# Attention with unscaled probabilities, streams that meet only their own keys, and output halves stored apart

## The chip, the cores and the metric

The kernel runs on one core of a Trainium2 chip. The metric is the device time of one execution in microseconds (us), taken as the median over several runs. Lower is better. A profile is one execution recorded by the hardware profiler.

## What is computed

One inference step of a two-layer encoder, for a prompt of 1024 frames and for 8 running streams of 16 new frames each (128 rows together). Layer one uses forgetting attention (causal, with a cumulative log-forget bias), layer two uses banded attention in chunks of 64 frames with a learned bias by distance. Each is followed by an output projection and a gated feed-forward block.

```python
def fox_attention_prompt(q, k, v, logf):            # 16 heads of 64, blocks of 128 queries
    s = einsum('bqhd,bkhd->bhqk', qb, k) * scale
    s = s + cq[..., :, None] - cum[..., None, :]
    s = where(key_pos[None, :] <= qpos[:, None], s, NEG_INF)
    p = softmax(s, axis=-1)
    return einsum('bhqk,bkhd->bqhd', p, v)
# streams: the same, each stream's 16 queries against its own 128 cached keys and its 16 new ones
h = h + merge_heads(attention(q, k, v, ...)) @ w_out
h = h + swiglu(rms_norm(h, g_ffn), w_gate_up, w_down)
```

## The kernel before

The program is a row of blocks, with a barrier of all engines between them: projections of the first layer, the first attention ("fox" in the names), its output projection ("aout"), feed-forward, projections of the second layer, the second attention ("band"), its output projection ("bout"), feed-forward. Every product is done to more than single-pass accuracy: an operand is split in a high and a low part, and the parts are multiplied apart.

**attention_block** (lines 783 to 1287) works head by head. A head has nine units: S, which holds the 128 stream rows, and eight prompt tiles of 128 queries, here t0 to t7. A prompt tile meets 1 to 8 key tiles in fox, 1 to 5 in band. S meets nine key tiles at once (the 8 streams' caches and the tile of new keys), and everything that is not a stream's own is masked by a third matmul of each piece (L1236, `own` against `others`). 18 units of two heads form a pair, and a hardware loop (`Fori`) goes over the pairs. Each engine runs its own program of steps, and unit n passes through it in stages that lag behind each other:

- TensorE (PE): `score(n)` at step n, into `sp_wide` or `sp_slim` in turns; four steps later `turn` transposes the probabilities, up to four tiles in one bank of `tp` (three banks); `values` six steps later multiplies them with the values, for two prompt tiles (a group) or for S. In a step the order is turn, score, values. The output bank `op` is the tail of `sp_wide`, so S's scores wait for it too.
- VectorE (DVE): `tensor_tensor_reduce` adds the bias and takes the row maximum (L1203); later a reciprocal (L1182) and, in fox, the scaling of the probabilities by it (L1185); `low` (L1174) makes the low part of the transposed probabilities; L1212 adds the two halves of the output.
- ScalarE (ACT): `high` (L1115), the exponential with its row sum (L1150), the copy of half the output (L1156), the high part of the values (L1126).
- GpSimd (POOL): in fox the bias of each unit (L1048, L1058, L1060) and the masked diagonals (L1033), in band the scaling (L1077); the low part of the values (L1024).
- SyncE (SP) issues the loads of each head (`load_head`), of the values of a pair (`load_values`) and the stores of the output (`store_head`), in the order of its program; each waits on semaphores.

**Turned** (lines 195 to 232) is the source of the output projection: it loads one token tile of the turned attention output (L219, 512 KB), and splits it (L224 on ACT, L228 on DVE). `dense_block` multiplies tile by tile, two chunks of 512 output columns, 24 matmuls for a tile and chunk.

## Time and profile before

| | us |
|---|---|
| median of 3 runs | 3515.49 |
| lowest and highest run | 3514.15, 3516.90 |
| span of the profiled execution | 3516.8 |
| first attention, 404 to 856 | 452 |
| first output projection, 866 to 968 | 102 |
| second attention, 2176 to 2540 | 364 |

The page gives PE as 91% busy, DVE 42%, ACT 33%, POOL 12% over the whole span. These averages mix dense blocks, in which PE never waits, with the two attentions, in which several engines share the work. So the stages are read apart: by windows of time, by the groups of instructions inside one window, and by the timeline of single instructions. In the timeline a record's end includes the way through the engine, and the next record of the same engine may begin some hundredths of a microsecond earlier.

### The profile page before, as it was taken

How to read it: one execution, taken by the hardware profiler on the slowest of the kernel's cores; microseconds unless marked ns; L12 is line 12 of the kernel's file. 1: busy time of each engine (PE TensorE's matmuls, PEld its weight loads, DVE VectorE, ACT ScalarE, POOL GpSimd, SP SyncE). 2: the span in 40 equal slices, each digit the busy share in tenths (PEclk: the TensorE clock that was granted, in tenths of full speed). 3: DMA queues.
4: the chain of work that ended last, by engine and by line, in shares of the span. 5: the costliest groups of instructions: out<-in, count | busy, mean ns of one | idle time of the engine just before them, and what ended most of it. 6: DMA issues, size and time to landing. Idle time of an engine off the chain costs nothing. (4 is left out here: it accounts for less than half of the span.)

```text
span 3516.8 us, 47851 instructions
## 1 busy us (share of the span) xinstructions
PE 3217.5 (91%) x16000; PEld 2680.0 (76%) x16000; DVE 1489.9 (42%) x2930; ACT 1174.2 (33%) x2540; POOL 423.7 (12%) x686
## 2 busy tenths in 40 slices
PE   8999577776999999999989997888699999999998
PEld 7877366665878888888878886777677888888887
DVE  3121388887243333333332221776634333333333
ACT  4232266665142211112223323777623122111122
POOL 0000245542000000000000001444300000000000
PEclk9999799998999999999999998999999999999999
DMA  4885343452441111111014884444322111111111
GB/s 153 200 250 166 137 153 141 153 178 74 125 156 60 48 36 36 36 36 52 19 51 144 241 213 160 158 157 160 106 84 78 37 51 56 36 36 36 36 36 54
DMA packets 329715, 363.82 MB, mean 103 GB/s; under 512 B 25200, under 2 KB 270976, under 8 KB 323344
## 3 DMA queue, kind: packets, MB, share of 16 engines
q1 hardware_dynamic: 329616, 362.52, 32.8%
q8 instruction: 60, 0.98, 0.1%
q14 instruction: 39, 0.32, 0.0%
HBM read 255.23 MB, written 120.98 MB: 107 GB/s over the span
## 5 line engine op out<-in xcount | busy, mean ns | idle before, releaser
L251 PE MATMUL ffn_gu<-ffn_gh,ffn_xh 128*128 128x512 f32 x1584 | 635.2, 401 | 0.0
L253 PE MATMUL ffn_gu<-ffn_gh,ffn_xl 128*128 128x512 f32 x1584 | 619.6, 391 | 0.0
L252 PE MATMUL ffn_gu<-ffn_gl,ffn_xh 128*128 128x512 f32 x1584 | 619.3, 391 | 0.0
L1517 DVE TENSOR_TENSOR all_h<-ffn_dn,all_h 128x1024 f32<-128x1024 f32 x198 | 242.4, 1224 | 354.3 <-PE ffn_dn L253 354.3
L1501 DVE TENSOR_TENSOR ffn_hid<-ffn_gu,ffn_gate 128x256 f32<-128x256 f32 x198 | 83.8, 423 | 722.2 <-ACT ffn_gate L1494 722.2
L1494 ACT ACTIVATE ffn_gate<-ffn_gu 128x256 f32<-128x256 f32 x198 | 75.7, 382 | 833.0 <-PE ffn_gu L253 833.0
L253 PEld LDWEIGHTS ffn_gu<-ffn_gh,ffn_xl 128*128 128x128 f32 x1584 | 298.0, 188 | 63.1
L252 PEld LDWEIGHTS ffn_gu<-ffn_gl,ffn_xh 128*128 128x128 f32 x1584 | 298.9, 189 | 56.8
L251 PEld LDWEIGHTS ffn_gu<-ffn_gh,ffn_xh 128*128 128x128 f32 x1584 | 298.4, 188 | 56.0
L251 PE MATMUL ffn_dn<-ffn_dh,ffn_hidh 128*128 128x512 f32 x792 | 308.4, 389 | 2.9 <-DVE ffn_hidl L1512 2.9
L253 PE MATMUL ffn_dn<-ffn_dh,ffn_hidl 128*128 128x512 f32 x792 | 309.0, 390 | 0.0
L252 PE MATMUL ffn_dn<-ffn_dl,ffn_hidh 128*128 128x512 f32 x792 | 308.2, 389 | 0.0
L1508 ACT ACTIVATE ffn_hidh<-ffn_tps 128x256 fp32r<-128x256 f32 x198 | 75.6, 382 | 438.1 <-PE ffn_tps L1472 438.1
L251 PEld LDWEIGHTS ffn_dn<-ffn_dh,ffn_hidh 128*128 128x128 f32 x792 | 148.7, 188 | 34.1 <-DVE ffn_hidl L1512 3.3
L251 PE MATMUL qkvw_acc<-qkvw_h,qkv_xh 128*128 128x512 f32 x432 | 173.5, 402 | 0.0
L251 PE MATMUL band_inw_acc<-band_inw_h,band_in_xh 128*128 128x512 f32 x432 | 172.7, 400 | 0.0
L253 PEld LDWEIGHTS ffn_dn<-ffn_dh,ffn_hidl 128*128 128x128 f32 x792 | 148.6, 188 | 30.9
L252 PEld LDWEIGHTS ffn_dn<-ffn_dl,ffn_hidh 128*128 128x128 f32 x792 | 148.7, 188 | 30.8
L1269 PE MATMUL fox_tp<-all_ident,fox_pr 128*128 128x128 f32 x720 | 125.4, 299 | 49.5 <-DVE fox_ptl L1174 29.3
L253 PE MATMUL qkvw_acc<-qkvw_h,qkv_xl 128*128 128x512 f32 x432 | 169.9, 393 | 0.0
L252 PE MATMUL qkvw_acc<-qkvw_l,qkv_xh 128*128 128x512 f32 x432 | 169.3, 392 | 0.0
L253 PE MATMUL band_inw_acc<-band_inw_h,band_in_xl 128*128 128x512 f32 x432 | 169.2, 392 | 0.0
(231 smaller groups left out, 6066.2 us busy)
## 6 DMA issues: line engine op xcount, KB each, us to landing
ffn_graw<-in_w_gate_up SPq DMA_DIRECT2D x40, 1024.0 KB, 7.5
ffn_draw<-in_w_down SPq DMA_DIRECT2D x22, 1024.0 KB, 4.9
fox_ks<-k_split SPq DMA_DIRECT2D x16, 1088.0 KB, 5.6
fox_ncb<-negcum SPq DMA_DIRECT2D x16, 1088.0 KB, 10.1
band_ks<-k_split SPq DMA_DIRECT2D x16, 1088.0 KB, 5.5
qkvw_raw<-in_w_a_in SPq DMA_DIRECT2D x5, 2048.0 KB, 9.6
out<-qkvw_stage SPq DMA_DIRECT2D x36, 256.0 KB, 3.2
q_high<-qkvw_th SPq DMA_DIRECT2D x72, 128.0 KB, 2.5
```

The costliest lines, as they stand in the source:

```text
L251: pe.matmul(out, xh, wh, start=first, stop=False)
L252: pe.matmul(out, xh, wl, start=False, stop=False)
L253: return pe.matmul(out, xl, wh, start=False, stop=last)
L1269: last = pe.transpose(tp[:, (base + k) % TB, b * P:(b + 1) * P], pr[slot_of[n]][:, (j + b) * P:(j + b + 1) * P], ident[:])
L1494: act.activation(gate[:], gu[:, t % 2, 0:GW], ACT.Silu).then_inc(gate_ready, 1)
L1501: dve.tensor_tensor(hid[:], gu[:, t % 2, GW:2 * GW], gate[:], ALU.mult).then_inc(hid_ready, 1)
L1508: act.activation(hidh[:].rearrange("p c n -> p (c n)"), tps[:, 0:GW], ACT.Copy).then_inc(hidh_ready, 1)
L1517: dve.tensor_tensor(h[:, t, :], dn[:].rearrange("p a n -> p (a n)"), h[:, t, :], ALU.add).then_inc(dn_used, 1)
```

## The change

In both attentions:

- The probabilities are not scaled. The row sums go into a new buffer `sums`, kept over the blocks, and `Turned` takes their reciprocals, spreads them over 64 columns of each head (POOL), turns them (PE, 8 transposes a tile) and multiplies them into the loaded output (DVE).
- S meets 2 key tiles in place of 9. `begin` computes each stream's scores against its own cache (8 matmuls of 32 moving columns, L1208), ACT and DVE add the two parts, and `score` turns the result back; the new keys are one more tile. `values` for S has 2 matmuls of 128 columns and 16 of 16 columns.
- The output leaves `op`, now a bank of its own, by one DVE copy (L1184) with both halves, which are stored apart. `Turned` loads two halves of 512 KB and POOL adds them.
- The values' high part moves from ACT to POOL; `split_values(hd+1)` stands in fox's POOL program between the bias of t5 and that of t6 of head hd, and waits for the load of the values when hd+1 is even.
- The loop over pairs is gone: all 16 heads are written out, S first in every head. Lags are shorter: turn 3 steps, values 5, output 6. In a PE step the order is turn, begin, values, score. The exponential of a unit stands in the same ACT step as its maximum in DVE's.
- fox loads the stream part of the bias by nine small transfers; SP's order is `load_values`, `load_head(hd + 2)`, `store_head(hd)`.

The core of the diff:

```diff
     def rsqrt(self, pool, t):
-        pass
+        s = t % 3
+        if t == 0:
+            pool.wait_ge(self.inv_ready, 1)
+        if t >= 2:
+            pool.wait_ge(self.spread, 2 * (t - 1))
+        pool.tensor_copy(self.rows[:, t % 2], self.inv[:, t, :].rearrange("p (u o) -> p u o", o=1)
+                         .to_broadcast([P, HEADS, HD])).then_inc(self.rows_ready, 1)
+        pool.wait_ge(self.loaded[s], 32 * (t // 3 + 1))
+        pool.tensor_tensor(out=self.raw[:, s, 0], in0=self.raw[:, s, 0], in1=self.raw[:, s, 1],
+                           op=ALU.add).then_inc(self.added, 1)
 
     def scaled(self, dve, t):
-        pass
+        if t == 0:
+            dve.reciprocal(self.inv[:], self.sums[:]).then_inc(self.inv_ready, 1)
+        dve.wait_ge(self.added, t + 1)
+        for half in range(2):
+            part = self.raw[:, t % 3, 0, 4 * half:4 * half + 4, :]
+            dve.wait_ge(self.spread, 2 * t + half + 1)
+            dve.tensor_tensor(part, self.ptr[:, half, :].rearrange("p (c n) -> p c n", c=4), part,
+                              ALU.mult).then_inc(self.scaled_done, 1)
...
     def fetch(self, sp, t):
-        if t >= 2:
-            sp.wait_ge(self.low_ready, t - 1)
-        sp.dma_start(self.raw[:, t % 2], self.src[:, t * P:(t + 1) * P].rearrange("(c p) n -> p c n", p=P)
-                     ).then_inc(self.loaded[t % 2], 16)
+        if t >= 3:
+            sp.wait_ge(self.low_ready, t - 2)
+        for u in range(2):
+            sp.dma_start(self.raw[:, t % 3, u], self.src[u, :, t * P:(t + 1) * P].rearrange("(c p) n -> p c n", p=P)
+                         ).then_inc(self.loaded[t % 3], 16)
...
+    UH = NT
+    N = HEADS * UH
+    GH = 1 + QT // 2
+    LT, LV, LO = 3, 5, 6
...
+                    sp.dma_start(f32(ks[b][:]), ks_d[hd]).then_inc(kq_loaded[b], 16)
+                    sp.dma_start(f32(q2[b][:, 0, :]), qh_d[hd]).then_inc(kq_loaded[b], 16)
+                    sp.dma_start(f32(q2[b][:, 1, :]), ql_d[hd]).then_inc(kq_loaded[b], 16)
...
 
                 def load_values(p):
-                    wait(sp, vl_done, 2 * NV * p)
+                    if p:
+                        sp.wait_ge(vl_done, 2 * p)
                     for at, n, src in v_parts:
-                        sp.dma_start(vraw[:, at:at + n, :], src(bass.ds(p * P, P))).then_inc(v_loaded, 16)
+                        sp.dma_start(vraw[:, at:at + n, :], src(slice(p * P, (p + 1) * P))).then_inc(v_loaded, 16)
+
+                def store_head(hd):
+                    sp.wait_ge(o_done, GH * (hd + 1))
+                    for u in range(2):
+                        sp.dma_start(out_d[u, hd * HD:(hd + 1) * HD, :], att[hd % 2][u * HD:(u + 1) * HD, :]
+                                     ).then_inc(att_stored[hd % 2], 16)
...
+                load_head(1)
+                for hd in range(HEADS):
+                    if hd % 2 and hd + 1 < HEADS:
+                        load_values((hd + 1) // 2)
+                    if hd + 2 < HEADS:
+                        load_head(hd + 2)
+                    store_head(hd)
...
+                def split_values(hd):
+                    b, at = hd % 2, hd % 2 * HD
+                    if b == 0:
+                        pool.wait_ge(v_loaded, 16 * len(v_parts) * (hd // 2 + 1))
+                    if hd >= 2:
+                        pool.wait_ge(pv_done, GH * (hd - 1))
+                    pool.tensor_copy(vs[b][:, :, 0:HD], vraw[:, :, at:at + HD]).then_inc(vh_done, 1)
+                    pool.wait_ge(vh_done, hd + 1)
+                    pool.tensor_tensor(out=vs[b][:, :, HD:P], in0=vraw[:, :, at:at + HD],
+                                       in1=f32(vs[b][:, :, 0:HD]), op=ALU.subtract).then_inc(vl_done, 1)
...
+                    for n in range(N):
+                        hd, i = head_of(n), tile_of(n)
+                        if i == S:
+                            diagonal(hd)
+                            if hd == 0:
+                                split_values(0)
+                        else:
+                            unit_bias(n)
+                        if i == 5 and hd + 1 < HEADS:
+                            split_values(hd + 1)
+                        if i == 6 and hd + 1 < HEADS:
+                            fox_streams(hd + 1)
...
+                for s in STEPS:
+                    n = turned_at(s)
+                    if n is not None:
+                        high(n, True)
+                    if 0 <= s - 1 < N:
+                        exp(s - 1)
+                    if n is not None:
+                        high(n, False)
+                    if begun_at(s) is not None:
+                        begun(begun_at(s))
...
+                for s in STEPS:
+                    if 0 <= s - 1 < N:
+                        maximum(s - 1)
+                    n = turned_at(s)
+                    if n is not None:
+                        low(n, True)
+                    if group_at(s, LO) is not None:
+                        out(group_at(s, LO))
+                    if n is not None:
+                        low(n, False)
+                    if begun_at(s) is not None:
+                        begun(begun_at(s))
...
+                def begin(hd):
+                    b, r = hd % 2, begun_round[hd]
+                    pe.wait_ge(kq_loaded[b], 48 * (hd // 2 + 1))
+                    if r >= TB:
+                        pe.wait_ge(tl_done, r - TB + 1)
+                    for x in range(STREAMS):
+                        at = S * P + x * NEW
+                        last = pe.matmul(tp[:, r % TB, 2 * NEW * x:2 * NEW * (x + 1)],
+                                         ks[b][:, (QT + x) * P:(QT + x + 1) * P], q2[b][:, :, at:at + NEW],
+                                         start=True, stop=True)
+                    last.then_inc(t_done, 1)
...
+                def values(g):
+                    hd, tiles = g // GH, tiles_of(g)
+                    v = vs[hd % 2]
+                    pe.wait_ge(vl_done, hd + 1)
+                    if g:
+                        pe.wait_ge(o_done, g)
+                    pe.wait_ge(tl_done, rounds_through(last_unit(g)))
                     if g % GH == 0:
-                        pe.wait_ge(vl_done, (2 * p + hh + 1) * NV)
-                    wait(pe, o_done, p * G + g)
-                    if scored is not None:
-                        pe.wait_ge(max_done, scored)
-                    pe.wait_ge(tl_done, p * R + rounds_through(last_unit[g]))
+                        for y, buf in enumerate(group_slots(g)):
+                            pe.matmul(op[:, 0:P], v[:, KT - 1, :], buf[:, P:2 * P], start=y == 0, stop=False)
+                        for x in range(STREAMS):
+                            for y, buf in enumerate(group_slots(g)):
+                                last = pe.matmul(op[:, x * NEW:(x + 1) * NEW], v[:, QT + x, :],
+                                                 buf[:, x * NEW:(x + 1) * NEW], start=False,
+                                                 stop=x == STREAMS - 1 and y == 1)
...
+                for s in STEPS:
+                    if turned_at(s) is not None:
+                        turn(turned_at(s))
+                    if begun_at(s) is not None:
+                        begin(begun_at(s))
+                    if group_at(s, LV) is not None:
+                        values(group_at(s, LV))
+                    if 0 <= s < N:
+                        score(s)
```

On DVE, in fox, these rows stood where the first head of a pair works on t4 to t6 (`pr` the probabilities, `bias` the bias, `sp_wide` and `sp_slim` the scores, `mneg` the negated maximum):

```order
L1203 ISA fox_pr1,fox_mneg<-fox_sp_wide,fox_bias0 128x640
L1203 ISA fox_mneg 128x1
L1212 TENSOR_TENSOR fox_att<-fox_sp_wide,fox_half_out 64x256
L1174 TENSOR_TENSOR fox_ptl<-fox_tp,fox_pth 128x2x128
L1182 RECIPROCAL fox_inv<-fox_rowsum 128x1
L1185 TENSOR_SCALAR fox_pr0<-fox_pr0,fox_inv 128x512
L1203 ISA fox_pr2,fox_mneg<-fox_sp_slim,fox_bias1 128x768
L1203 ISA fox_mneg 128x1
L1174 TENSOR_TENSOR fox_ptl<-fox_tp,fox_pth 128x3x128
L1182 RECIPROCAL fox_inv<-fox_rowsum 128x1
L1185 TENSOR_SCALAR fox_pr1<-fox_pr1,fox_inv 128x640
L1203 ISA fox_pr3,fox_mneg<-fox_sp_wide,fox_bias0 128x896
```

And these stand there now, at t6 and t7 and the start of the next head:

```order
L1174 ISA fox_pr,fox_mneg<-fox_score,fox_bias 128x896
L1174 ISA fox_mneg 128x1
L1148 TENSOR_TENSOR fox_ptl<-fox_tp,fox_pth 128x4x128
L1184 COPY fox_att0<-fox_op 128x256
L1148 TENSOR_TENSOR fox_ptl<-fox_tp,fox_pth 128x128
L1154 TENSOR_TENSOR fox_whole_st<-fox_tp,fox_half_st 128x128
L1174 ISA fox_pr,fox_mneg<-fox_score,fox_bias 128x1024
L1174 ISA fox_mneg 128x1
L1148 TENSOR_TENSOR fox_ptl<-fox_tp,fox_pth 128x4x128
L1148 TENSOR_TENSOR fox_ptl<-fox_tp,fox_pth 128x2x128
L1174 ISA fox_pr,fox_mneg<-fox_score,fox_bsm1 128x256
```

The reciprocal and the scaling are gone. In one step now stand the maximum of a unit, the low parts of the unit two before it (its second part last) and, before the maximum of t7, the sum of the next head's stream scores (L1154).

On PE, in fox, before, where S of the second head is multiplied with the values (`sth` and `stl` S's probabilities, `pth` and `ptl` a group's, `vs` the values):

```order
L1233 MATMUL fox_sp_slim<-fox_ks1,fox_qh1 128x512
L1234 MATMUL fox_sp_slim<-fox_ks1,fox_ql1 128x512
L1233 MATMUL fox_sp_slim<-fox_ks1,fox_qh1 128x256
L1234 MATMUL fox_sp_slim<-fox_ks1,fox_ql1 128x256
L1269 MATMUL fox_tp<-all_ident,fox_pr4 128x128 x3
L1233 MATMUL fox_sp_wide<-fox_ks1,fox_qh1 128x512
L1234 MATMUL fox_sp_wide<-fox_ks1,fox_ql1 128x512
L1233 MATMUL fox_sp_wide<-fox_ks1,fox_qh1 128x384
L1234 MATMUL fox_sp_wide<-fox_ks1,fox_ql1 128x384
L1258 MATMUL fox_sp_wide<-fox_sth,fox_vs1 128x128
L1258 MATMUL fox_sp_wide<-fox_stl,fox_vs1 128x128
L1258 MATMUL fox_sp_wide<-fox_sth,fox_vs1 128x128
```

And now (`fox_score` the scores, `fox_op` the output bank), from the end of the values of t6 and t7:

```order
L1271 MATMUL fox_op<-fox_pth,fox_vs0 128x128
L1271 MATMUL fox_op<-fox_ptl,fox_vs0 128x128
L1230 MATMUL fox_score<-fox_ks1,fox_q21 128x512
L1231 MATMUL fox_score<-fox_ks1,fox_q21 128x512
L1241 MATMUL fox_tp<-all_ident,fox_pr 128x128 x2
L1254 MATMUL fox_op<-fox_sth,fox_vs1 128x128
L1254 MATMUL fox_op<-fox_stl,fox_vs1 128x128
L1257 MATMUL fox_op<-fox_sth,fox_vs1 128x16
L1257 MATMUL fox_op<-fox_stl,fox_vs1 128x16
L1257 MATMUL fox_op<-fox_sth,fox_vs1 128x16
```

The scores stood ahead of the values and stand behind them now; 16 of S's 18 value matmuls have 16 moving columns in place of 128, and their number is the same.

## Rows read from the trace of the kernel before

**Rows 1.** Windows: from:to, length; busy PE, PEld, DVE, ACT, POOL; PEclk, DMA share, GB/s.
```profile
404.00:856.00 452.00, 347.42 (x2176) 300.16 (x2176) 382.26 (x896) 277.35 (x656) 225.25 (x352) 0.90 0.41 146
866.00:968.00 102.00, 100.84 (x432) 82.93 (x432) 30.76 (x41) 16.58 (x23) 0.00 (x0) 0.97 0.43 126
2176.00:2540.00 364.00, 293.32 (x2016) 259.84 (x2016) 250.54 (x752) 268.93 (x689) 155.52 (x224) 0.95 0.44 148
```

**Rows 2.** Timeline, POOL, first attention: start us, us, work; every second mask of the diagonal.
```profile
506.89 1.09 POOL L1033 TENSOR_SCALAR_AFFINE_SELECT fox_diag<-fox_ncb 128x1024 f32<-128x1024 f32 x1 [0.23 <-POOL fox_bias L1060]
...
562.65 1.09 POOL L1033 TENSOR_SCALAR_AFFINE_SELECT fox_diag<-fox_ncb 128x1024 f32<-128x1024 f32 x1 [0.23 <-POOL fox_bias L1060]
```

**Rows 3.** Groups by form, DVE, 572 to 628 us: xcount | busy us, mean ns | idle.
```profile
L1174 DVE TENSOR_TENSOR fox_ptl<-fox_tp,fox_pth 128x512 fp32r<-128x512 f32 x13 | 8.9, 684 | 2.2 <-ACT fox_pth L1115 2.1
...
L1212 DVE TENSOR_TENSOR fox_att<-fox_sp_wide,fox_half_out 64x256 f32<-64x256 f32 x8 | 3.3, 416 | 0.5 <-ACT fox_half_out L1156 0.2
...
L1203 DVE CUSTOM_DVE_ANT_0 fox_pr<-fox_sp_slim,fox_bias 128x1024 f32<-128x1024 f32 x1 | 1.2, 1205 | 0.0
...
L1203 DVE CUSTOM_DVE_ANT_0 fox_pr<-fox_sp_slim,fox_bias 128x128 f32<-128x128 f32 x2 | 0.6, 278 | 0.0
```

**Rows 4.** The same view, ACT: exponential, reading of its sum, copy of turned scores.
```profile
L1115 ACT ACTIVATE fox_pth<-fox_tp 128x512 fp32r<-128x512 f32 x12 | 7.0, 595 | 7.9 <-PE fox_sp_wide L1258 4.4 <-PE fox_tp L1269 3.3
...
L1150 ACT ACTIVATION_READ_ACCUMULATOR fox_pr<-fox_pr,fox_mneg 128x1 f32 x18 | 3.4, 192 | 0.0
...
L1150 ACT ACTIVATE fox_pr<-fox_pr,fox_mneg 128x1024 f32<-128x1024 f32 x2 | 2.3, 1150 | 1.9 <-DVE fox_mneg L1203 1.9
...
L1150 ACT ACTIVATE fox_pr<-fox_pr,fox_mneg 128x128 f32<-128x128 f32 x2 | 0.8, 401 | 0.3 <-DVE fox_mneg L1203 0.3
```

**Rows 5.** Timeline, PE, first attention: consecutive matmuls, in three places.
```profile
607.03 0.41 PE L1258 MATMUL fox_sp_wide<-fox_pth,fox_vs 128*128 128x256 f32 x1
607.24 0.41 PE L1258 MATMUL fox_sp_wide<-fox_ptl,fox_vs 128*128 128x256 f32 x1
...
612.24 0.28 PE L1258 MATMUL fox_sp_wide<-fox_ptl,fox_vs 128*128 128x256 f32 x1
612.36 0.22 PE L1258 MATMUL fox_sp_wide<-fox_pth,fox_vs 128*128 128x128 f32 x1
612.42 0.28 PE L1258 MATMUL fox_sp_wide<-fox_ptl,fox_vs 128*128 128x128 f32 x1
...
616.14 0.28 PE L1258 MATMUL fox_sp_wide<-fox_sth,fox_vs 128*128 128x128 f32 x1
616.25 0.28 PE L1258 MATMUL fox_sp_wide<-fox_stl,fox_vs 128*128 128x128 f32 x1
```

**Rows 6.** DMA issues: xcount, KB each, median us from issue to landing.
```profile
fox_vraw<-in_cache_a_v SPq DMA_DIRECT2D x8, 512.0 KB, 5.6
...
aoutw_at<-attn_turned SPq DMA_DIRECT2D x9, 512.0 KB, 4.1
```

**Rows 7.** Groups by form, POOL, 572 to 628 us.
```profile
L1060 POOL TENSOR_SCALAR fox_bias<-fox_diag,fox_cqh 128x128 f32<-128x128 f32 x17 | 7.8, 458 | 1.5 <-DVE fox_mneg L1203 1.2 <-POOL fox_cqh L1036 0.3
...
L1024 POOL TENSOR_TENSOR fox_vs<-fox_vraw,fox_vs 128x384 fp32r<-128x384 f32 x4 | 4.0, 1003 | 0.4 <-ACT fox_vs L1126 0.4
...
L1058 POOL TENSOR_SCALAR fox_bias<-fox_ncb,fox_cqh 128x768 f32<-128x768 f32 x2 | 1.8, 908 | 2.2 <-DVE fox_mneg L1203 2.2
```

**Rows 8.** Timelines where the first projection begins: SP, PE and ACT.
```profile
856.87 0.40 SPq L219 DMA_DIRECT2D aoutw_at<-attn_turned  x1
...
866.39 0.80 PE L251 MATMUL aoutw_acc<-aoutw_h,aout_xh 128*128 128x512 f32 x1 [14.52 <-DVE aout_xl L228]
...
868.72 1.06 ACT L224 ACTIVATE aout_xh<-aoutw_at 128x1024 fp32r<-128x1024 f32 x1 [0.51 <-DMA aoutw_at<-attn_turned]
```

**Rows 9.** Groups by form, DVE, 572 to 628 us: the scaling of the probabilities.
```profile
L1185 DVE TENSOR_SCALAR fox_pr<-fox_pr,fox_inv 128x768 f32<-128x768 f32 x2 | 2.9, 1438 | 0.1
...
L1185 DVE TENSOR_SCALAR fox_pr<-fox_pr,fox_inv 128x1024 f32<-128x1024 f32 x3 | 2.3, 762 | 0.1
```

More of the change, by code:

```diff
@@ L312, in dense_block @@
             if turned_src is not None:
-                src = Turned(pw, turned_src, xh, xl)
+                src = Turned(pw, turned_src, xh, xl, ptr, ident, sums)
             else:
@@ L796, in width @@
     def width(i):
[L797 removed]
+        return 2 if i == S else (i + 1 if fox else min(i, BAND_TILES) + 1)
     def first_key(i):
[L800 to L808 removed]
@@ L856, in attention_block, with parts_of, turned_at @@
-    samples = [n for n, (_, i) in enumerate(order) if i == S]
-    values_step = [n + VALUES + ((n + VALUES) % U in samples) for n in last_unit]
-    out_step = [v + OUT - VALUES for v in values_step]
-    assert all(b > a for a, b in zip(values_step, values_step[1:])) and values_step[-1] < values_step[0] + U
+        return i + 1 - width(i)
+    def parts_of(i):
+        return [(j, min(4, width(i) - j)) for j in range(0, width(i), 4)]
+    def turned_at(s):
+        return s - LT if 0 <= s - LT < N else None
@@ new lines, in begun_at, with group_at @@
+    def begun_at(s):
+        return head_of(s + 1) if 0 <= s + 1 < N and tile_of(s + 1) == S else None
+    def group_at(s, lag):
+        n = s - lag
+        if not 0 <= n < N or n % UH % 2:
+            return None
+        return GH * head_of(n) + n % UH // 2
+    STEPS = range(-1, N + LO)
+    round_of, begun_round, r = {}, {}, 0
+    for s in STEPS:
+        n = turned_at(s)
+        if n is not None:
+            for j, _ in parts_of(tile_of(n)):
+                round_of[n, j] = r
+                r += 1
+        if begun_at(s) is not None:
+            begun_round[begun_at(s)] = r
+            r += 1
@@ L928, in pairs_loop @@
-        def pairs_loop(eng, steps):
-            steps(0, range(U), True)
-            with eng.Fori(1, PAIRS) as p:
-                steps(p, range(U), False)
-            steps(PAIRS - 1, range(U, out_step[-1] + 1), False)
-        def groups_at(p, first, step, steps_of):
-            for g, s in enumerate(steps_of):
-                if s == step:
-                    yield g, p
-                elif s == step + U and not first:
-                    yield g, p - 1
+        bias_done, diag_made, bsm_part, bsm_made = (ph.sem(x) for x in ("bias_done", "diag_made", "bsm_part", "bsm_made"))
@@ L1090, in band_pair @@
-                def band_pair(p, last=False):
-                    for n in range(U):
-                        if n == first_of_head[1] - 4:
-                            band_bias(p, 1)
-                        if n == U - 4 and not last:
-                            band_bias(p + 1, 0)
-                        normalise(p, n)
-                        values_low(p, n + NORM)
-                pair = fox_pair if fox else band_pair
-                if not fox:
-                    band_bias(0, 0)
@@ L1103, in _ @@
-                pair(0)
-                with pool.Fori(1, PAIRS - 1) as p:
-                    pair(p)
-                pair(PAIRS - 1, last=True)
+                pool.memset(own[:], 0.0).then_inc(own_made, 1)
+                pool.wait_ge(own_made, 1)
+                view = own[:].rearrange("p (b k) -> p b k", b=STREAMS)
+                pool.affine_select(out=view, in_=view, compare_op=ALU.is_ge, fill=NEG, base=0,
+                                   pattern=[[-NEW, STREAMS], [0, NEW]], channel_multiplier=1).then_inc(own_made, 1)
```

602 lines of the change are left out of this document (263 added, 339 removed).

## The prediction

> **What bounds the kernel now.** The windows of the three stages come first [rows 1]. In fox DVE is busy 382 of 452 us, PE 347, at a granted clock of 0.90: DVE is nearest to its limit. In band nobody is: PE 293, ACT 269, DVE 251 of 364. In the projection PE is busy 100.8 of 102. So a gain in an attention comes from shorter chains between engines, and any PE work or late start added to a projection costs its full time. The second view is the period of a pair: two masks of the diagonal with one between them are 55.8 us apart in fox [rows 2], 27.9 for a head; 16 heads are 446 us and about 6 are fill and drain. Band gives (364 - 6) / 16 = 22.4 us a head. The third is what single instructions take, which the chains below use [rows 3, 4, 5, 7].
>
> **What is removed.** The scaling took DVE 0.76 us for 1024 columns and 1.44 us for 768 [rows 9], so not its width but something beside it set its time. The Trainium skill ("SBUF — State Buffer", Who interferes with whom) says that a DVE instruction in a two-port mode and a GpSimd instruction lock each other out; the longer time of the narrower row agrees. By that rule the scaling's going speeds POOL as well, and it speaks against `Turned`: `low` reads two SBUF tensors there while POOL now adds, and by the rule each may wait up to a POOL instruction, 1 to 4 us a projection. The sum below leaves that out. DVE's own work is no longer a limit after the change, so I don't price the removal by work; I ask what chain is left.
>
> **The new chain, in steps.** I take one head of fox in steady state. A maximum of w tiles takes DVE 0.28 us at one tile and 1.21 at eight, so 0.13 more a tile; a low part 0.68 for four tiles and, as a maximum of the same width, 0.28 for one; the output copy 0.42 as the addition it replaces (nearest row, same columns) [rows 3]. An exponential takes ACT 0.40 to 1.15 and the reading of its sum 0.19; the copy of a high part 0.60 for four tiles and, taken as DVE's, 0.28 for one [rows 4]. I take off 0.05 for overlap of records and add 0.04 for a handover.
>
> In the four steps in which the transposed tile (t4 to t7) has a second part, DVE's next maximum waits for: maximum, exponential and reading, high of the second part, low of the second part. With the maximum of t6: 1.10 + 0.04 + 1.17 + 0.30 + 0.27 = 2.87, and 0.26 for the streams' sum: 3.13. With t7: 3.37. With S: 2.2. With t0: 2.14. Together 10.8 us. The other five steps go by DVE's work (maximum, low, output): 1.27, 0.80, 1.51, 1.79, 1.61, together 7.0. That would be 17.8 us a head.
>
> PE holds up two of these five, because the values now stand ahead of the scores and one bank holds the output. At full clock a matmul of 256 columns takes 0.12 us to the next start; one of 128 takes 0.06 behind one of 256, and 0.11 in the streams' row of matmuls of 128 [rows 5]. For those of 16 columns, which no row shows, the bounds are 0.06 and 0.11; I take 0.11, the row of the same place and order. Count from the start of the step with the maximum of t0. The output copy of t4/t5 ends at 3.4; the values of t6/t7 (14 of 0.12 and two more) end at 5.3; the scores of t3 (0.46) are complete at 5.95, where DVE could have begun at 4.2. DVE takes that maximum, a low part and the copy of t6/t7, until 7.45; then 18 stream matmuls, 2.0 us, the scores of t4, 0.68, and the way through the engine: 10.4, where DVE could have begun at 7.45. The two holds cost 1.75 and 2.95: **22.5 us a head**.
>
> The Trainium skill ("TensorE: Matmul & The Clock Gate", LDWEIGHTS) gives a weight load a time by its 128 columns, however few move after it, which fits the 0.11; its section Back-to-back issue gap gives a narrow matmul by itself some 25 ns, and by that the streams' values would take 0.5 us a head in place of 2.0 and the sum be 48 us less.
>
> **A wait that the change adds in fox.** POOL's `split_values` for an even head stands between the bias of t5 and of t6 of the head before, and waits for values that SP issues only after `store_head` of the head before that. In the count above: the copy of t6/t7 ends at 7.45; SP issues two stores and three loads, about 2 us; the last lands 5.6 us after its issue [rows 6]: 14.9. The high and low parts of 1088 columns, at 1.18 and 2.6 ns a column, take 4.1 us; the bias of t6 0.91 + 0.46 [rows 7]: 20.4. DVE needs it at 13.8. Queued behind the split on POOL are the biases of t6 and t7 and the next streams' bias; DVE, and through it everyone, waits **6.6 us**, seven times (for heads 2, 4 to 14). In between PE idles for some 7 us. In band no bias stands behind the split, and the values have a whole head's time: nothing.
>
> **Clock.** At the reduced clock of 1.2 GHz matmuls of 256 columns start 0.21 apart in place of 0.12 [rows 5], and fox had 0.90 on the mean [rows 1]. The 5.0 us of values and scores in the two holds would double. I allow 0.5 us a head in fox, 0.3 in band.
>
> Fox: 16 x 22.5 + 7 x 6.6 + 16 x 0.5 + 6 fill + 4 (the first values are split before the first prompt bias) = 424, against 452: **-28**.
>
> **Band.** Same steps with at most five tiles and a second part of one: 2.66, 2.40, 1.75, 1.41 and 1.25, 0.80, 1.51, 1.79, 1.47, together 15.0. Holds: t6/t7's values take 1.3, so the scores of t3 are there at 4.7 instead of 3.5; the streams' values and t4's scores at 9.1 instead of 6.2. 15.0 + 1.2 + 2.9 = 19.2; with the clock 19.5. 16 x 19.5 + 6 = 318, against 364: **-46**. POOL's scaling and ACT's spreading of the bias, half output and values go with it; they lay beside the chain.
>
> **Projections, twice.** Before, the first matmul came 9.5 us after the first load was issued, and the second tile landed 11.8 us after [rows 8], behind 3 MB (0.5 + 2 of weights + 0.5). Now 4 MB stand there: 15.2 us. DVE handles the second tile before it touches the weights, so the first matmul waits for it: addition on POOL 1024 x 2.6 ns = 2.7, two multiplications of 512 columns 1.3, two low parts of weights 1.3, `low` of 1024 columns 1.2 (all at the 0.68 of 512, less overlap), together 6.5: 21.7 us in place of 9.5, **+12.2**. Then 8 transposes a tile at 0.11 come ahead of PE's matmuls for seven of the nine tiles: **+6**. Per tile PE now takes 24 x 0.23 + 0.9 = 6.4 us (432 matmuls in 100.8 [rows 1]); POOL 3.8, DVE 3.3, and a buffer comes round in 10.5 us for two tiles, so none holds PE. Together +18.2, twice: **+36**.
>
> Everything else is untouched. The nine small bias loads add some 4 us of issue on SP a head, which has 22. The barrier and the stores (two in place of one) cost nothing that the fill doesn't hold. The load grows little: about 4.1 MB a head, at 22 us 186 GB/s against 146 now at a share of 0.41.
>
> Sum on the profiled span: 3516.8 - 28 - 46 + 36 = 3479. The span is 1.3 us above the median, so 3477 in the median's terms. I add 8 us, since every term of the chains is a lower count of waits: **3485 us**.
>
> **Rivals.**
> *The reduced clock stays.* The 6.6 us stalls and the short idle times leave PE at 1.2 GHz in the two holds of every fox head: 5.0 us more for each, less the 0.5 allowed: 16 x 4.5 = 72, 3557 us, slower than before. It decides from 31 / 16 = 1.9 us a head, that is with two fifths of the holds at the low clock. For it: a mean of 0.90 before, with shorter idle times. Against: PE is 70% occupied outside the stalls, where it was 60%.
> *The values arrive in time, or the stall hides.* If the load lands 6 us earlier or the split needs less, 7 x 6.6 = 46 fall away: 3439. For it: SP's own issue times are estimates. Against: the order of its program.
> *Narrow matmuls start closer.* At the lower bound, 0.06, the streams' values take 1.1 us in place of 2.0, and 32 x 0.9 = 29 fall away: 3456. For it: the 0.06 of rows 5. Against: that one's weights were loaded under a wider matmul, and none of the 16 has such cover.
> *The holds of PE don't bite*: 16 x (4.7 + 4.1) = 141 less, 3344, the lowest. Against it speak the order rows of PE: values ahead of scores, one bank.
> *The scaling does not leave the bound*, that is DVE's work before was hidden: excluded in fox by 382 of 452 us.
>
> **How the numbers follow.** Forecast 3485, between 3460 and 3520: 0.42. Narrow matmuls, 3450 to 3460: 0.08. Clock, 3520 to 3570: 0.22. No stall, 3405 to 3450: 0.20. No holds, below 3405: 0.05; beyond 3570: 0.03. The 80% range takes most of the clock case and of the one without stall: 3415 to 3555. A measurement can tell 0.2%, 7 us. The forecast case lies below 3508.5 with 0.34 of its 0.42; so faster: 0.34 + 0.08 + 0.20 + 0.05 = 0.67. Within 0.2%: its other 0.08 and the lowest 0.04 of the clock case, 0.12. Slower than 3522.5: 0.18 + 0.03 = 0.21.
>
> **What would show it.** In the changed profile: fox heads in pairs of about 22.5 and 29 us, DVE waiting for POOL's bias of t6 some 6 to 7 us, seven times; PE waiting for L1184 ahead of values; stream matmuls of 16 columns 0.11 apart; in the projections the first matmul some 22 us after the first load, 6.4 us a tile in the first chunk. Wrong it is if DVE never waits for a bias, if L1257 starts closer than 0.11, or if the granted clock of fox lies below 0.85.

## The result, and the profile after

| | before | changed |
|---|---|---|
| median of 4 runs, us | 3514.82 | 3579.72 |
| lowest and highest, us | 3513.67, 3516.90 | 3574.73, 3583.52 |
| span of the profiled execution, us | 3516.8 | 3578.5 |

The changed kernel is slower: ratio 1.0184, with a 95% interval of 1.0169 to 1.0198. I had forecast 3485, with a range of 3415 to 3555. The table compares the stages of the two profiled executions, each from the first load that it issues to that of the next stage. A stage of mine is that of before plus the terms of the prediction.

| stage, us | before | forecast | changed | off by |
|---|---|---|---|---|
| to the first attention | 396.3 | 396.3 | 398.1 | +1.8 |
| first attention | 460.6 | 432.6 | 445.5 | +12.9 |
| its output projection | 112.2 | 130.4 | 159.4 | +29.0 |
| feed-forward | 855.0 | 855.0 | 858.2 | +3.2 |
| projections of layer two | 343.8 | 343.8 | 343.2 | -0.6 |
| second attention | 375.4 | 329.4 | 349.4 | +20.0 |
| its output projection | 111.8 | 130.0 | 159.9 | +29.9 |
| feed-forward | 861.7 | 861.7 | 864.8 | +3.1 |
| span | 3516.8 | 3479 | 3578.5 | +99 |

Both attentions are faster than before, by 15 and 26 us, as forecast in sign and too small in size. The two projections lose 95 us, where I had 36. That is 59 us more than forecast, the larger part of the miss.

The windows answer to [rows 1], with the same columns: the first attention, the second, and the first half of the first projection and the rest of it.

```profile
405.00:842.00 437.00, 331.61 (x2096) 297.64 (x2096) 229.94 (x592) 209.56 (x513) 210.39 (x320) 0.84 0.45 146
...
2212.00:2552.00 340.00, 289.55 (x1936) 259.35 (x1936) 206.11 (x592) 187.37 (x513) 74.29 (x96) 0.90 0.53 175
...
868.00:936.00 68.00, 53.25 (x209) 42.43 (x210) 23.21 (x30) 6.34 (x6) 19.28 (x11) 0.84 0.44 124
936.00:1001.00 65.00, 62.85 (x281) 51.68 (x279) 16.36 (x23) 6.94 (x11) 0.00 (x0) 1.00 0.35 100
```

DVE has gone from 382 us to 230 in fox, so the scaling did leave. But the granted clock of PE is 0.84 where it was 0.90, and 0.90 where it was 0.95: more of PE's work runs at 1.2 GHz. In the projection's first 68 us PE is idle for 15; before it was idle for 0.4 of the first 51.

**The projection.** The timeline of PE, then of DVE, at tiles 1 and 2 of the first chunk (start, length, and in brackets the idle time and what ended it):

```profile
875.65 1.04 PE L243 MATMUL aoutw_ptr<-all_ident,aoutw_rows 128*128 128x128 f32 x8
878.92 0.51 PE L282 MATMUL aoutw_acc<-aoutw_h,aout_xh 128*128 128x512 f32 x1 [2.23 <-DVE aout_xl L259]
...
886.09 1.03 PE L243 MATMUL aoutw_ptr<-all_ident,aoutw_rows 128*128 128x128 f32 x8
889.36 0.68 PE L282 MATMUL aoutw_acc<-aoutw_h,aout_xh 128*128 128x512 f32 x1 [2.23 <-DVE aout_xl L259]
```

```profile
862.62 4.21 DVE L276 TENSOR_TENSOR aoutw_l<-aoutw_raw,aoutw_h 128x512 fp32r<-128x512 f32 x2
...
886.80 1.29 DVE L232 TENSOR_TENSOR aoutw_at<-aoutw_ptr,aoutw_at 128x512 f32<-128x512 f32 x2 [7.33 <-PE aoutw_ptr L243]
888.00 1.30 DVE L259 TENSOR_TENSOR aout_xl<-aoutw_at,aout_xh 128x1024 fp32r<-128x1024 f32 x1
```

PE turns the reciprocals of tile 3 (886.09) only after the matmuls of tile 1. DVE's program has the multiplication of tile 3 (L232, 886.80) ahead of the low part of tile 2 (L259, 888.00), so that low part, of a tile that had been multiplied 9 us before, waits for PE's transposes, and PE's next matmul waits for the low part. The round repeats about every 10.4 us (878.92 to 889.36), with 2.1 to 3 us of idle PE, and behind most of these holes 6 to 8 matmuls start 0.43 us apart in place of 0.23: the granted clock is at its lower level there. None of this stands in my working.

**The first attention.** DVE around the end of a stalled head and in the next one; `fox_bias` of 896 columns is t6's:

```profile
607.05 0.69 DVE L1174 CUSTOM_DVE_ANT_0 fox_pr<-fox_score,fox_bias 128x512 f32<-128x512 f32 x1 [2.07 <-PE fox_score L1231]
...
612.95 0.82 DVE L1174 CUSTOM_DVE_ANT_0 fox_pr<-fox_score,fox_bias 128x640 f32<-128x640 f32 x1 [4.51 <-PE fox_score L1231]
...
622.78 1.09 DVE L1174 CUSTOM_DVE_ANT_0 fox_pr<-fox_score,fox_bias 128x896 f32<-128x896 f32 x1 [5.72 <-POOL fox_bias L1043]
...
642.54 0.82 DVE L1174 CUSTOM_DVE_ANT_0 fox_pr<-fox_score,fox_bias 128x640 f32<-128x640 f32 x1 [3.97 <-PE fox_score L1231]
...
730.52 1.09 DVE L1174 CUSTOM_DVE_ANT_0 fox_pr<-fox_score,fox_bias 128x896 f32<-128x896 f32 x1 [9.05 <-issue]
...
744.47 0.69 DVE L1174 CUSTOM_DVE_ANT_0 fox_pr<-fox_score,fox_bias 128x512 f32<-128x512 f32 x1 [2.07 <-PE fox_score L1231]
...
748.89 0.82 DVE L1174 CUSTOM_DVE_ANT_0 fox_pr<-fox_score,fox_bias 128x640 f32<-128x640 f32 x1 [3.02 <-PE fox_score L1231]
...
765.90 0.69 DVE L1174 CUSTOM_DVE_ANT_0 fox_pr<-fox_score,fox_bias 128x512 f32<-128x512 f32 x1 [2.07 <-PE fox_score L1231]
```

And what t6's bias waited for, on SP and then on POOL:

```profile
608.47 1.09 SPq L987 DMA_DIRECT2D attn_turned<-fox_att  x2
609.61 0.77 SPq L982 DMA_DIRECT2D fox_vraw<-out  x1
610.42 1.52 SPq L982 DMA_DIRECT2D fox_vraw<-in_cache_a_v  x1
611.98 1.76 SPq L982 DMA_DIRECT2D fox_vraw<-out  x1
```

```profile
617.75 1.09 POOL L1010 CAST fox_vs<-fox_vraw 128x1088 fp32r<-128x1088 f32 x1 [11.73 <-DMA fox_vraw<-out]
618.93 2.49 POOL L1012 TENSOR_TENSOR fox_vs<-fox_vraw,fox_vs 128x1088 fp32r<-128x1088 f32 x1
621.40 0.91 POOL L1042 TENSOR_SCALAR fox_bias<-fox_ncb,all_cq 128x768 f32<-128x768 f32 x1
622.28 0.37 POOL L1043 TENSOR_SCALAR fox_bias<-fox_diag,all_cq 128x128 f32<-128x128 f32 x1
```

This is the chain of the prediction, step for step: stores, loads, split, bias. The wait came seven times, 5.28 to 9.05 us, 49.5 in all. The maximum of t3 waits 2.06 us for its scores and that of t4 3.02 to 4.9. Where the releaser reads "issue" (730.52), the profile names none; e2, further down, shows that this wait is of the same kind.

### The profile page after: what moved, and what is told of

It reads as the page before. It is cut to its first block and busy times, and to the rows that moved or that the text cites. A ratio compares the mean times of both kernels' runs of the same rounds, so it can differ in the third digit from the quotient of the medians.

```text
span 3578.5 us, 43068 instructions
## 1 busy us (share of the span) xinstructions
PE 3243.7 (91%) x15984; PEld 2709.1 (76%) x15984; DVE 1326.0 (37%) x2504; ACT 1021.2 (29%) x2216; POOL 386.5 (11%) x559
## 5 line engine op out<-in xcount | busy, mean ns | idle before, releaser
L283 PE MATMUL band_inw_acc<-band_inw_l,band_in_xh 128*128 128x512 f32 x432 | 168.7, 391 | 0.0
## 6 DMA issues: line engine op xcount, KB each, us to landing
qkvw_raw<-in_w_a_in SPq DMA_DIRECT2D x5, 2048.0 KB, 10.4
```

What stands on the lines that cost most here:

```text
L283: pe.matmul(out, xh, wl, start=False, stop=False)
```

## Experiments

Each kernel stands beside runs of the kernel before on the same chip, whose medians were 3517.85 (e1 to e4), 3516.85 (e5, c1, c2, e7) and 3516.70 (c3, c4, e8). "Against the changed kernel" means against its median of 3579.7, or stage by stage. A stage's time is that of one profiled execution, and it scatters: the first attention, whose code is the same in the changed kernel, e1 and e5, took 445.5, 448.8 and 440.0 us there, the second 349.4, 346.5 and 349.5. A second output bank for `op` was not tried.

**e1, the projection's order.**

```diff
-                                if t + 2 < NT:
-                                    src.scaled(dve, t + 2)
                                 if t + 1 < NT:
                                     src.low(dve, t + 1)
+                                if t + 2 < NT:
+                                    src.scaled(dve, t + 2)
```

> The changed kernel with one swap: in the first chunk of the two output projections DVE makes the low part of tile t+1 before it multiplies tile t+2 by the reciprocals. In the changed kernel a tile of that chunk takes 10.4 us: PE turns the reciprocals of tile t+1, then waits 2.23 us for DVE's low part of tile t, which stands behind the multiplication that waits for just these transposes, and then runs 8 or 9 matmuls at the reduced clock. Theory 1 (that loop is the cost): a tile takes 6.4 to 7 us, PE does not wait for L259 after the first tile, 8 x 3.7 = 30 us less in each projection, about 3520 us in all. Theory 2 (the load of two halves is the cost, POOL waits 7 us for each): a tile stays above 9 us, at most 10 us less in each, 3560 us or more. Theory 3 (the reduced clock would be there anyway): the holes go, the slow matmuls stay, 18 us less in each, about 3544 us.

Measured: 3521.6 us, ratio to before 1.0012 (1.0002 to 1.0022), 58 us less than the changed kernel. The projections take 133.1 and 132.9 in place of 159.4 and 159.9, which is 53 of the 58. PE, then DVE:

```profile
870.39 0.79 PE L282 MATMUL aoutw_acc<-aoutw_h,aout_xh 128*128 128x512 f32 x1 [12.76 <-DVE aout_xl L259]
...
878.13 1.03 PE L243 MATMUL aoutw_ptr<-all_ident,aoutw_rows 128*128 128x128 f32 x8
...
884.51 1.03 PE L243 MATMUL aoutw_ptr<-all_ident,aoutw_rows 128*128 128x128 f32 x8
```

```profile
878.84 1.29 DVE L232 TENSOR_TENSOR aoutw_at<-aoutw_ptr,aoutw_at 128x512 f32<-128x512 f32 x2 [3.76 <-PE aoutw_ptr L243]
...
881.25 3.46 DVE L259 TENSOR_TENSOR aout_xl<-aoutw_at,aout_xh 128x1024 fp32r<-128x1024 f32 x1 [0.53 <-ACT aout_xh L255]
```

PE turns every 6.4 us and waits no more. Theory 1 holds; theory 2 falls, since the load of two halves is still there and hidden; theory 3 falls, since the slow matmuls went with the holes.

**e5, the start as well.** e1, and `src.scaled(dve, 1)` behind `chunk_low` in the two output projections.

> The changed kernel with the swap of DVE's low part and multiplication in the first chunk (e1), and besides, in the output projections, DVE's multiplication of tile 1 moved behind the low parts of the first weights, so that nothing of tile 0 stands behind it. In the changed kernel and in e1 the first matmul starts 24.3 us after the first load. Theory 1 (it waits for the landing and the addition of tile 1, which DVE handles first): it starts 12 to 15 us after the first load, 9 to 12 us less in each projection, 20 in all against e1, about 3500 us. Theory 2 (the weights land that late anyway, behind the 1 MB of tile 0): the first matmul moves by under 3 us, 3515 to 3522.

Measured: 3500.5 us, 0.9954 (0.9937 to 0.9970), 21 less than e1. The first matmul starts 12.5 us after the stage's first load (833.7 and 846.2), and the stage takes 124.6 and 123.2, which is 8.5 and 9.7 less than in e1. Theory 1, at the low end of its 9 to 12.

**e2, the values early.**

```diff
-                    if hd % 2 and hd + 1 < HEADS:
-                        load_values((hd + 1) // 2)
+                    if hd % 2 == 0 and hd + 2 < HEADS:
+                        load_values(hd // 2 + 1)
```

> The changed kernel with one move on SP: the values of the next pair are loaded before the keys of head hd+2 and before the store of head hd (hd even), instead of after that store, one head later. Seven waits of DVE for the bias of t6, 5.3 to 9.1 us, stood in the changed kernel. Theory 1 (they come from the late load alone): all seven go, and with them part of the reduced clock, 50 to 65 us less in the first attention, 3515 to 3530 us in all; the pair of heads goes from 54 us to 45 to 47. Theory 2 (the queue only shifts: keys and biases of the next head, issued behind the values, are late instead): DVE or PE waits for keys or a bias of the next head, 10 to 30 us less, 3550 to 3570. Band: no change, within 3 us, by both.

Measured: 3532.8 us, 1.0042 (1.0025 to 1.0059), 47 less than the changed kernel; the first attention takes 400.3 in place of 445.5. The seven waits are gone and nothing came in their place. The second attention is 5.1 us shorter, more than the 3 that I allowed; part of that lies within the scatter given above. But the clock came back in small part only, 0.87 in the first attention where the changed kernel has 0.84:

```profile
403.00:790.00 387.00, 325.03 (x2096) 291.49 (x2096) 230.04 (x591) 209.20 (x513) 211.02 (x320) 0.87 0.50 162
```

```profile
447.77 0.82 DVE L1174 CUSTOM_DVE_ANT_0 fox_pr<-fox_score,fox_bias 128x640 f32<-128x640 f32 x1 [4.07 <-PE fox_score L1231]
...
588.54 0.82 DVE L1174 CUSTOM_DVE_ANT_0 fox_pr<-fox_score,fox_bias 128x640 f32<-128x640 f32 x1 [3.02 <-PE fox_score L1231]
```

In 10 of 15 heads the maximum of t4 still waits 4.1 to 4.8 us for its scores, in the others 3.02. So the stalls cost about what they last (45.2 us of 49.5), and most of the reduced clock is not their doing. Theory 1 for the wait, not for the clock.

**e3, scores ahead of values.** In PE's step `score(s)` stands before `values(...)`.

> The changed kernel with one swap on PE, in both attentions: in a step the scores stand ahead of the values. DVE waited for the scores of t3 2.06 us in every head of fox and 1.56 in band, for those of t4 3.0 to 4.9. Theory 1 (these are holds by the order on PE): both waits fall below 1 us; fox 16 x 4.5 = 72 us less, if no new wait comes, band 16 x 4 = 64 less; since PE's own work in band is some 260 us at full clock, and in fox the stalls for the bias stay, I expect 50 to 110 in all, 3470 to 3530 us. Theory 2 (PE's work is the bound, the order only moves the wait): the waits come back at other units, under 20 us less, 3560 to 3580.

Measured: 3523.5 us, 1.0018 (1.0008 to 1.0029), 56 less than the changed kernel: 24 in the first attention (421.7) and 30 in the second (318.9). DVE's waits:

```profile
439.43 0.42 DVE L1148 TENSOR_TENSOR fox_ptl<-fox_tp,fox_pth 128x256 fp32r<-128x256 f32 x1 [1.60 <-ACT fox_pth L1111]
...
443.40 0.56 DVE L1148 TENSOR_TENSOR fox_ptl<-fox_tp,fox_pth 128x384 fp32r<-128x384 f32 x1 [2.47 <-ACT fox_pth L1111]
```

The waits for the scores of t3 and t4 are gone, 5.1 us a head, and in their place stand two for the turned tiles, 1.60 and 2.47 or more: the values that no longer hold the scores now hold the next turn. A clean head becomes 1.5 us shorter in both attentions (19.98 in place of 21.43, 17.68 in place of 19.24), not 5. The seven stalls, moreover, grow from 49.5 to 57.5 us in all, since the head is faster and the values come no sooner. Theory 1 in direction, a third of its size in fox and half in band.

**e4, wide matmuls for the streams.**

```diff
-                                last = pe.matmul(op[:, x * NEW:(x + 1) * NEW], v[:, QT + x, :],
-                                                 buf[:, x * NEW:(x + 1) * NEW], start=False,
+                                last = pe.matmul(op[:, 0:P], v[:, QT + x, :],
+                                                 buf[:, 0:P], start=False,
```

> The changed kernel, but the 16 matmuls of a head that multiply the streams' own cached values move 128 columns in place of 16 (all add into the same 128 output columns, so the attention output of the stream rows is not the one wanted; all else is computed). In the changed kernel they start 0.11 us apart, and the granted clock often falls in the midst of them, after which they take 0.21. Theory 1 (few moved columns let the clock fall there): each still takes 0.11, the clock stays up, DVE's wait for the scores of t4 is 3.0 in all heads, 25 to 40 us less in all, 3540 to 3555. Theory 2 (the clock falls for the 1.3 us idle time before them or the stalls, not for their width): no change, 3575 to 3585. Theory 3 (width costs time): slower, up to 16 x 16 x 0.05 x 2 = 25 us.

Measured: 3561.8 us, 1.0121 (1.0104 to 1.0138), 18 less than the changed kernel. By stages it is 10.9 in the first attention and 6.1 in the second, little more than their scatter. What told it is the changed kernel's row of stream matmuls beside DVE's waits here:

```profile
608.68 0.28 PE L1254 MATMUL fox_op<-fox_stl,fox_vs 128*128 128x128 f32 x1
...
609.43 0.26 PE L1257 MATMUL fox_op<-fox_sth,fox_vs 128*128 128x16 f32 x1
609.54 0.29 PE L1257 MATMUL fox_op<-fox_stl,fox_vs 128*128 128x16 f32 x1
609.68 0.36 PE L1257 MATMUL fox_op<-fox_sth,fox_vs 128*128 128x16 f32 x1
609.89 0.36 PE L1257 MATMUL fox_op<-fox_stl,fox_vs 128*128 128x16 f32 x1
610.11 0.36 PE L1257 MATMUL fox_op<-fox_sth,fox_vs 128*128 128x16 f32 x1
```

```profile
553.16 0.82 DVE L1174 CUSTOM_DVE_ANT_0 fox_pr<-fox_score,fox_bias 128x640 f32<-128x640 f32 x1 [3.02 <-PE fox_score L1231]
...
604.26 0.83 DVE L1174 CUSTOM_DVE_ANT_0 fox_pr<-fox_score,fox_bias 128x640 f32<-128x640 f32 x1 [3.02 <-PE fox_score L1231]
```

In the changed kernel the starts go from 0.11 to 0.21 apart in the middle of the row, at 609.68: the granted clock falls from 2.4 to 1.2 GHz while PE is back to back, and stays down for the scores of t4 and t5. With 128 moving columns, in the first attention from the head at 497 on, not one maximum of t4 waits longer than 3.02. The idle time before the row (1.3 us) is the same in both. In the second attention it is otherwise: with 128 columns the clock still falls inside the row in 5 heads of 16, where it was 6, and 11 of 15 maxima of t4 wait 3.3 to 4.4 us. So theory 3 falls, since a stream matmul costs 0.11 whether it moves 16 columns or 128. Theory 1 holds in the first attention; its "3.0 in all heads" and its 25 to 40 us do not come true, and theory 2 is not refuted here: the idle time may act as well. The width by itself is tried in c3.

**c1, the four moves together.**

> All four moves together, everything computed: DVE's low part first and the multiplication of tile 1 late in the projections (e5), the values of a pair loaded early (e2), the scores ahead of the values on PE (e3). Measured apart, e1 brought 58 us, e2 47, e3 56, and the late multiplication should bring 20. If they are independent: 3580 - 58 - 20 - 47 - 56 = 3399 us. If e2 and e3 overlap (the heads that no longer stall come up against PE's own work, and the clock falls as often), up to 40 less is gained: 3440. Either is faster than the kernel before (3518) by over 2%.

Measured: 3395.5 us, 0.9646 (0.9630 to 0.9662), against 3399 by the sum. The gains add up. In the first attention they give 79 us where e2 and e3 gave 45 and 24 apart: e3 alone had made the seven stalls 8 us longer, and here there are none.

**c2, the first split late.**

> c1 with one more move on POOL: in the first head of the first attention the values are split behind the biases of t0 to t2, not ahead of them. In the changed kernel DVE waited 6.9 us for the bias of t0 of the first head, since the splitting waits for the values and takes 3.6 us. Theory 1: that wait goes, 5 to 7 us less than c1. Theory 2 (the wait moves to S's values, which PE needs 5 steps later): under 2 us.

Measured: 3396.4 us, 0.9643 (0.9622 to 0.9665), no difference from c1. The wait of 7.5 us for the bias of t0 became 1.1, and the maximum of t3 waits 4.3 instead, for its bias, which POOL makes behind the split:

```profile
413.89 2.48 POOL L1015 TENSOR_TENSOR fox_vs<-fox_vraw,fox_vs 128x1088 fp32r<-128x1088 f32 x1
416.35 0.59 POOL L1045 TENSOR_SCALAR fox_bias<-fox_ncb,all_cq 128x384 f32<-128x384 f32 x1
416.91 0.38 POOL L1046 TENSOR_SCALAR fox_bias<-fox_diag,all_cq 128x128 f32<-128x128 f32 x1
```

Theory 2 in size; but the wait moved to the bias of t3, not to S's values.

**c3, wide, with everything computed.** The turned probabilities of S are written with a stride of 144 columns into buffers set to zero once, and matmul x moves the window of 128 columns from 128x.

```diff
+        sth = ph.sb("sth", [P, 2, STREAMS * (P + NEW)], F32R)
...
+                    out.append(buf[:].rearrange("p k (x w) -> p k x w", w=P + NEW)[:, :, :, 0:NEW])
...
+                                last = pe.matmul(op[:, 0:P], v[:, QT + x, :],
+                                                 buf[:, 0, x * P:(x + 1) * P], start=False,
```

> c1 with the streams' values made wide and everything computed: the turned probabilities of S lie in blocks of 144 columns with zeros between them, and each of the 16 matmuls moves 128 columns, of which 16 are not zero. In e4 the same width, on the changed kernel, brought 18 us. Theory 1 (the granted clock falls in the streams' narrow matmuls): the clock of both attentions rises from 0.90 and 0.89 to 0.93 or more, 10 to 25 us less than c1: 3370 to 3386 us. Theory 2 (with the scores ahead and the stalls gone PE is busy enough, or the clock falls elsewhere): within 5 us of c1, 3390 to 3401.

Measured: 3364.8 us, 0.9564 (0.9548 to 0.9580), 31 less than c1. Windows of the two attentions, c1 and then c3:

```profile
407.00:764.00 357.00, 311.58 (x2096) 277.79 (x2096) 227.86 (x592) 205.17 (x513) 210.57 (x320) 0.90 0.54 177
2101.00:2412.00 311.00, 280.52 (x1935) 252.74 (x1935) 201.38 (x592) 182.92 (x513) 73.91 (x96) 0.91 0.58 190
```

```profile
404.00:744.00 340.00, 292.74 (x2096) 257.23 (x2096) 224.90 (x592) 205.23 (x513) 210.88 (x320) 0.97 0.57 187
2079.00:2374.00 295.00, 264.49 (x1935) 236.43 (x1934) 201.16 (x592) 182.33 (x513) 74.14 (x96) 0.97 0.61 200
```

The clock goes from 0.90 and 0.91 to 0.97; the attentions take 348.9 and 305.6 in place of 366.6 and 321.0. The idle time before the row is 0.7 us in nearly every head of both kernels. In c1 the starts go from 0.11 to 0.21 inside the row in 8 of 32 heads, in c3 in none. Theory 1, and by more than I expected: the width is shown as a cause.

**e7, e8 and c4: a shift of addresses.** The diff of e7 is one line in the kernel before, `unused = al.sb("unused", [P, NT, HEADS])`; e8 has `[P, 256]`; c4 is c3 with `[P, 256 - NT * HEADS]` (112 columns) behind `sums`.

> The kernel before with one unused buffer of 576 bytes a partition, of the size and at the place of the changed kernel's sums, so that every later buffer has the same shift of its address as in the changed kernel. Each feed-forward block takes 3.1 us longer in the changed kernel, 858.1 and 864.8 in place of 855.0 and 861.7, though nothing in it is changed and PE is never idle in it. Theory 1 (the addresses): both blocks take 858 and 865 here, and the whole 6 us more, 3523 us. Theory 2 (the position of the loops in a longer program, or anything else): 855 and 862, 3517.

> The kernel before with an unused buffer of 1024 bytes a partition in place of the 576 of e7. Theory 1 (a shift that is a multiple of 1024 bytes costs nothing): feed-forward blocks of 855.0 and 861.7 as in the kernel before, 3517 us. Theory 2 (any shift of the addresses costs): 857.8 and 864.8 as in e7, 3523 us.

> c3 with 448 unused bytes a partition behind the 576 of the sums, so that later buffers are shifted by 1024 bytes against the kernel before. Theory 1 (the feed-forward blocks lose their 3 us each to a shift that is no multiple of 1024): both take 855 and 862 again, and the whole 6 us less than c3. Theory 2 (any shift costs this, or the multiple has to be larger): no change against c3.

Measured: e7 3522.96 us, 1.0019 (1.0010 to 1.0029), feed-forward 857.8 and 864.8. e8 3517.8, 1.0000 (0.9990 to 1.0009), 855.0 and 861.8. c4 3357.9, 0.9543 (0.9527 to 0.9559), 854.7 and 861.7 where c3 has 857.9 and 865.1. The groups of PE in 1055 to 1400 us, the kernel before and then e7:

```profile
L251 PE MATMUL ffn_gu<-ffn_gh,ffn_xh 128*128 128x512 f32 x328 | 131.3, 400 | 0.0
...
L252 PE MATMUL ffn_gu<-ffn_gl,ffn_xh 128*128 128x512 f32 x329 | 128.4, 390 | 0.0
```

```profile
L251 PE MATMUL ffn_gu<-ffn_gh,ffn_xh 128*128 128x512 f32 x326 | 131.4, 403 | 0.0
L252 PE MATMUL ffn_gu<-ffn_gl,ffn_xh 128*128 128x512 f32 x326 | 128.1, 393 | 0.0
```

Theory 1 three times. The matmuls of `ffn_gu` are 3 ns longer on the mean in two of their three kinds (L251, L252) and 2 ns shorter in the third (L253, 391 and 389); with 1584 of each kind that is the 6 us. Those of `ffn_dn` are as before. c4 is the best version: 4.6% faster than the kernel before, 6.2% faster than the changed one.

## Why the prediction was wrong

**Projections, the first chunk: +6 forecast, +32 measured.** This step failed. I counted what each engine does for a tile (PE 6.4 us, POOL 3.8, DVE 3.3), found all below PE, and concluded that none holds PE. I did not follow the order on DVE against the order on PE, as I did for the attentions. e1 gives the term: 26.3 and 27.0 us in the two projections. What is left in e1 is 6.4 us a tile, the figure I had.

**Projections, the start: +12.2 forecast, +14.9 measured.** The cause was right (the second tile, handled first; e5). The size was off by 2.7 us, and one row has it: two low parts at 862.62 took 4.21 us, which take 0.68 each undisturbed. The first took 2.77 beside POOL's addition (862.49 to 864.84), the second 1.52 beside the copy that POOL makes next. In e1 a low part at 881.25 took 3.46 us, where 1.2 is usual, beside POOL's addition at 881.24. The rule that I set beside the sum and left out of it (the Trainium skill, "SBUF — State Buffer", Who interferes with whom) agrees with both rows, and its price, 2.8 us, was in the 1 to 4 that I gave.

**Stall for the bias of t6: 46 forecast, 49.5 measured.** Seven times, in the heads named, through the chain named. One term in it was wrong in size: the stores and loads took SP 5.3 us to issue (608.47 to 613.74), not 2, and the last landed at 617.7, 5.8 after its issue began. From the maximum of t0 (601.28) the bias was ready after 21.4 us, where I had 20.4, and DVE wanted it after 15.8 in this head, where I had 13.8. e2 confirms it.

**Chain of a head.** Fox without stall and at full clock: 21.4 us (744.47 to 765.90), forecast 22.5. Band 19.24, forecast 19.2. The two holds of PE: 2.06 and 3.02 in fox, forecast 1.75 and 2.95. Without the holds the chain is 16.4 and 14.7 us, where I had 17.8 and 15.0, so my count of it was too long and the holds too short; that band's sum comes out exactly is partly luck. The rival that they don't bite is refuted; e3 shows that without them a clean head is only 1.5 us shorter, since the turned tiles then come late. The streams' matmuls start 0.11 apart at full clock, and as far apart at 128 columns (e4, c3): the price of 0.11 was right and the rival of narrow matmuls wrong.

**Clock: 0.5 and 0.3 us a head forecast, 1.65 and 1.16 left over.** This term was mis-sized. From the maximum of t3 in the second head (444.22) to that in the last (816.70) are 372.5 us; 14 clean heads are 299.9 and the stalls 49.5, and 23.1 are left. In band it is 285.6 less 269.4. Together some 27 us over. What is left over I put down to the clock; it is not measured by itself. I had named the rival that the reduced clock stays, and put it down to idle time. e2 has no stalls and still 10 slow heads of 15. Inside the row of stream matmuls the starts go from 0.11 to 0.21 in these heads of the two attentions: 7 and 6 of 16 in the changed kernel, 2 and 5 with wide matmuls (e4), 3 and 4 with the scores ahead, where the idle time before the row is 0.7 us in place of 1.3 (e3), 4 and 4 in c1, none in c3. So the narrow matmuls bring part of it, shown by c1 against c3; the idle time seems to bring another part, which no run separates from the order. The narrow matmuls are back to back, so the busy time of PE shows nothing of them. My 70 and 60% of occupied PE, by which I argued against this rival, stand on no row: the windows have 76% in the first attention now and 77% before.

**Fill and start.** Fox 21.6 us where I had 10, band 13.9 where I had 6: the loads of the first streams' bias (2.7 us of DVE's wait) and the split ahead of the first bias (6.9, priced at 4) are some 6 of the 12 in fox; besides, the first head's row of stream matmuls runs at 0.21 from its start in both attentions. The rest was not traced. The one other order that I tried for the split gave nothing (c2).

**Feed-forward, +6.** Named untouched, and it is, but for the addresses of its buffers (e7, e8).

Against my sum of 3479 for the profiled span these are: projections 58.9, clock 26.6, fills 19.5, stalls 3.3, fox heads -17.3, band heads 0.6, feed-forward 6.3, the rest of the table 1.2; together 99. The rival that ended slower, at 3557, had the right sign for a reason that gives 27 of them. With the projections at my 130 us each the span would have been 3520, close to before: the rest of the miss takes the gain away, and the projections turn it into a loss.

## What to carry to other kernels

When a new step joins a pipeline, write down for each engine what stands ahead of what, and walk the ring once: an engine can be half idle and still hold up all others, if its program puts the step that waits ahead of the one that is waited for. Load what a later step will need as soon as its buffer is free, not where the program mentions it. Replacing wide matmuls by narrow ones saved nothing here, since both start 0.11 us apart, and cost clock in the rows and behind them.

## What the runs showed of the hardware

- Matmuls of 128 weight columns start 0.11 us apart with 16 moving columns and with 128. With 0.7 us of idle time before the row, the granted clock fell in the middle of it in 8 of 32 heads in the narrow form (c1) and in none in the wide form (c3): 0.90 against 0.97 over the first attention, worth 33 us in the two attentions. With 1.3 us of idle time it fell in 13 of 32 heads in the narrow form (the changed kernel) and in 7 in the wide form (e4).
- An unused buffer of 576 bytes a partition, ahead of the blocks' own buffers, made two feed-forward blocks 2.8 and 3.1 us longer; one of 1024 bytes did not. The time is in `ffn_gu`'s matmuls (403 and 393 ns against 400 and 390). What in the addresses decides was not tried.
- A DVE subtraction of two SBUF tensors, started together with or just behind POOL's addition of 1024 columns (2.35 us), took 2.77 us in place of 0.68 (changed kernel, 862.62) and 3.46 in place of 1.21 (e1, 881.25).
